# First norm of a conditioned RG-LRU block: scale folded into the input weights, shift into a bias per channel

## The reference

```python
cond = jax.nn.silu(c)
mod = cond @ ada_w[0] + ada_b[0]              # 6 * 1024 columns
sh1, sc1, g1, sh2, sc2, g2 = jnp.split(mod, 6, axis=-1)
hn = rmsnorm(x, norm1_g[0]) * (1.0 + sc1[:, None, :]) + sh1[:, None, :]
# rglru_mixer(hn, ...)
u = h @ w_in
gate_br, x_br = u[..., :LRU_WIDTH], u[..., LRU_WIDTH:]
x_br = causal_dwconv(x_br, conv_w, conv_b)    # 4 taps
# two gates: sigmoid of x_br @ wa, x_br @ wx, block by block of 128 channels
# a = exp(-8 r softplus(-lam)), b = sqrt(1 - a^2) * (i * x_br), hs = scan of a, b over the tokens
y = hs * jax.nn.gelu(gate_br, approximate=True)
```

## Time and profile before

| | us |
|---|---|
| median of three runs | 1261.25 |
| lowest and highest | 1256.77, 1261.7 |
| the profiled execution | 1262.1 |
| its span, first to last instruction | 1260.4 |
| TensorE busy | 1093.1 (87%) |
| VectorE busy | 768.6 (61%) |
| ScalarE busy | 650.0 (52%) |
| GpSimd busy | 611.9 (49%) |

### The profile page before, as it was taken

One profiled execution on the slowest core, in us unless ns is written; L12 is line 12 of the kernel. 1 busy time (PEld: TensorE's weight loads), 2 busy tenths in 40 slices (PEclk: granted clock), 3 DMA queues, 4 the chain that ended last, 5 costly groups with the idle time before them and its releaser, 6 DMA issues. The chain is left out here.

```text
span 1260.4 us, 18928 instructions
## 1 busy us (share of the span) xinstructions
PE 1093.1 (87%) x4857; PEld 850.4 (67%) x4858; DVE 768.6 (61%) x1198; ACT 650.0 (52%) x900; POOL 611.9 (49%) x665
## 2 busy tenths in 40 slices
PE   2797999999999997379999992599799999999991
PEld 2686788888888885368888871476466666766660
DVE  3477866667657664536677778356456655656541
ACT  3988766776677666322222212255556655555541
POOL 0061726637447340022567767146555655666553
PEclk9788999999999999689999995699999999999996
DMA  9550334433343312661445627857687887776751
GB/s 362 194 193 29 107 102 135 154 117 121 118 156 118 117 51 83 220 231 69 152 179 189 234 118 267 271 191 252 222 297 245 288 299 245 261 250 231 246 168 51
DMA packets 130871, 231.00 MB, mean 183 GB/s; under 512 B 24104, under 2 KB 91776, under 8 KB 129296
## 3 DMA queue, kind: packets, MB, share of 16 engines
q1 hardware_dynamic: 88976, 118.15, 28.2%
q0 software_dynamic: 23632, 62.49, 13.5%
q10 hardware_dynamic: 18224, 49.90, 11.6%
HBM read 175.87 MB, written 91.31 MB: 212 GB/s over the span
## 5 line engine op out<-in xcount | busy, mean ns | idle before, releaser
L1687 PE MATMUL po<-w_dn,e_ah 128*128 (+1 forms) x312 | 147.1, 616 | 16.9 <-issue 8.9
L1666 PE MATMUL pl<-w_hi,e_xh 128*128 (+1 forms) x312 | 140.9, 452 | 11.8 <-DVE e_xl L1577 6.3
L1210 PE MATMUL po<-wo_hi,b_yh 128*128 128x512 f32 x256 | 105.0, 410 | 28.0 <-DVE wo_lo L1024 28.0
L1668 PE MATMUL pl<-w_hi,e_xl 128*128 (+1 forms) x312 | 124.7, 400 | 0.0
L1667 PE MATMUL pl<-w_lo,e_xh 128*128 (+1 forms) x312 | 124.0, 397 | 0.0
L558 DVE SCALAR_TENSOR_TENSOR XB<-xu,v_cols,XB 128x512 f32<-128x512 f32 x96 | 90.1, 939 | 43.2 <-ACT XB L336 39.5
L1687 PEld LDWEIGHTS po<-w_dn,e_ah 128*128 128x128 f32 x312 | 57.9, 195 | 80.0 <-issue 80.0
L1377 POOL TENSOR_TENSOR e_ob<-e_obs,e_fg 128x1024 f32<-128x1024 f32 x38 | 91.1, 2397 | 32.2 <-ACT e_obs L1495 32.2
L674 PE MATMUL pg<-hT_hi,wg_hi 128*128 128x512 f32 x256 | 103.1, 403 | 0.0
L1211 PE MATMUL po<-wo_lo,b_yh 128*128 128x512 f32 x256 | 101.6, 397 | 0.0
L1212 PE MATMUL po<-wo_hi,b_yl 128*128 128x512 f32 x256 | 101.6, 397 | 0.0
(11 more groups left out here) (287 smaller groups left out, 2637.4 us busy)
## 6 DMA issues: line engine op xcount, KB each, us to landing
e_xg<-hn_slots ACTq DMA_DIRECT2D x40, 512.0 KB, 5.4
e_xa<-x_slots ACTq DMA_DIRECT2D x38, 512.0 KB, 3.8
stg<-in_ada_w_dram POOLq DMA_DIRECT2D x32, 512.0 KB, 4.2
w_raw<-in_moe_w_down_dram SPq DMA_DIRECT2D x16, 1024.0 KB, 7.3
w_raw<-in_moe_w_gate_dram SPq DMA_DIRECT2D x32, 384.0 KB, 4.3
w_raw<-in_moe_w_up_dram SPq DMA_DIRECT2D x32, 384.0 KB, 5.7
n_ada<-in_ada_w_dram ACTq DMA_DIRECT2D x4, 2048.0 KB, 18.4
hn_slots<-in_x_dram SPq DMA_DIRECT2D x16, 512.0 KB, 5.4
```

The source lines that it names most:

```text
L1210: nc.tensor.matmul(po[u][:, hcols], yh[u][:, tok], wo_hi[:, k, hcols], start=(k == 0), stop=False)
L1666: nc.tensor.matmul(gu[:], xh[:, tok], hi, start=(k == 0), stop=False)
L1668: last = nc.tensor.matmul(gu[:], xl[:, tok], hi, start=False, stop=(k == KD - 1))
L1687: last = nc.tensor.matmul(dst, ah[:, k * P:(k + 1) * P], rows, start=(k == 0), stop=(k == KF - 1))
```

## The change

hn @ W is written as (x * rstd) @ (scale * W) + shift @ W. So the tiles no longer get scale and shift; the input weights of each channel are multiplied by scale, and shift @ W becomes a bias of 128 numbers per channel and branch. In particular:

- zT and finish_group are gone. ScalarE copies the turned bank straight to the high part (high), VectorE subtracts it from the bank for the low part (low). A bank is free for the next turn only when low is done.
- Per channel and branch VectorE makes weights times shift (into a scratch that lies over stg for channel 0 and over GE later), weights times scale in place (scale_weights), and a reduction over k of the first (bias_sums). TensorE sums that over the partitions (bias_column, one product of width one), ScalarE copies it to SBUF. The bias enters in the copy of px to xu and in the gelu.
- convert waits for the scaled weights. The gelus wait until the scratch over GE is free.
- SP loads the condition rows and the first channel's weights first and holds the x tiles back until the third quarter of the table has landed. The small decay constants move ahead of the tiles.
- Tiles 4 to 15 are scaled in place by VectorE (tensor_scalar, 128x1024) and turned by a transpose in place of the product with a diagonal. There are four diagonals in place of two.
- TensorE turns five tiles ahead of the first projection (twelve before), three behind each of the first two, five behind the first g projection. A projection of fresh tokens waits once for its whole group. The first gates wait for all 16 low parts. GpSimd starts its table loads when the g bias sums of channel 0 are done.

```diff
 def turn(it):
     pe.wait_ge(diag_ready, 2 * it + 2)
     if it >= 2:
-        pe.wait_ge(zT_ready, it - 1)
+        pe.wait_ge(lo_ready, it - 1)
...
+                if it < FIRST_SCALED:
+                    last = nc.tensor.matmul(dst, rows, diag[:, it % NDIAG], start=True, stop=True)
+                else:
+                    last = nc.tensor.transpose(dst, rows, cst["ident"][:])
...
             def convert(br, j):
-                act.wait_ge(raw_in[br], 16 * (j + 1))
+
+                act.wait_ge(prepared, 6 * j + (2 if br == "x" else 5))
                 nc.scalar.activation(whi[br][:], raw[br][:], ACT.Copy).then_inc(hi_done[br], 1)
...
+            def low(it):
+                dve.wait_ge(hi_ready, it + 1)
+                toks = slice(it * P, (it + 1) * P)
+                nc.vector.tensor_tensor(hT_lo[:, :, toks], pt[it % 2][:].rearrange("p (k n) -> p k n", k=KD),
+                                        hT_hi[:, :, toks].bitcast(F32), ALU.subtract).then_inc(lo_ready, 1)
...
+                nc.vector.tensor_tensor(shifted[not at_least(j, 1)][:], raw[br][:], by_key(shift), ALU.mult).then_inc(prepared, 1)
+                dve.wait_ge(prepared, i + 1)
+                nc.vector.tensor_tensor(raw[br][:], raw[br][:], by_key(scale), ALU.mult).then_inc(prepared, 1)
...
+                nc.vector.tensor_reduce(part[:], shifted[not at_least(j, 1)][:].rearrange("p k n -> p n k"), AX.X, ALU.add).then_inc(prepared, 1)
...
                     if before:
                         finish(hh)
+                    if h == 0 and not last:
+                        if before:
+                            dve.wait_ge(y_ready, hh)
+                        scale_weights("x", j + 1)
+                        bias_sums("x", j + 1)
                     if h == 1:
                         mod_row(j)
+                        if not last:
+                            dve.wait_ge(y_ready, hh)
+                            scale_weights("g", j + 1)
+                            bias_sums("g", j + 1)
...
                     else:
-                        pe.wait_ge(zT_ready, NT - 1)
+                        pe.wait_ge(lo_ready, NT)
```

More of the change, by code:

```diff
@@ L213, in _ @@
             load_bias(0)
-            for it in range(XR, NT):
+            sp.wait_ge(ada_in[2], 16)
+            for it in range(NT):
                 load_tile(it)
@@ L290, in gates_out @@
+            high(7)
+            squares(8)
+            squares(9)
             def gates_out(c, n, j):
@@ L311, in decay, with gelus @@
                 nc.scalar.activation(M[:], A[:], ACT.Square).then_inc(sq_ready, 1)
-            def gelus(hh, first):
+            def gelus(hh, j, first, later):
+                if later is not None:
+                    act.wait_ge(prepared, later)
                 for n in range(NH):
@@ L510, in _ @@
             nc.vector.tensor_scalar(sp_t[:, 0], lam, -1.0, 0.0, ALU.mult, ALU.max).then_inc(s_b, 1)
+            weigh(4)
             dve.wait_ge(s_b, 9)
@@ L516, in _ @@
             nc.vector.tensor_scalar(gb, gb, 0.5, None, ALU.mult).then_inc(s_b, 1)
+            weigh(5)
+            diagonal(0)
+            diagonal(1)
+            weigh(6)
+            weigh(7)
+            diagonal(2)
+            diagonal(3)
+            low(0)
+            low(1)
+            columns()
+            scale_weights("x", 0)
+            low(2)
+            bias_sums("x", 0)
+            low(3)
+            diagonal(4)
+            low_weights("x", 0)
+            diagonal(5)
+            low(4)
+            diagonal(6)
+            low(5)
+            scale_weights("g", 0)
+            diagonal(7)
+            low(6)
+            bias_sums("g", 0)
+            low_weights("g", 0)
+            low_gates(0)
+            low(7)
+            diagonal(8)
+            diagonal(9)
             def finish(hh):
@@ L583, in body @@
                         scan_input(hh - 1)
+                    if begins and h == 0:
+                        low(8)
+                        low(9)
+                        diagonal(10)
+                        diagonal(11)
                     low_xb(c, 0)
```

253 lines of the change are left out of this document (132 added, 121 removed).

## The result

The changed kernel takes 1279.7 us (median of four runs, 1277.49 to 1284.12), where the kernel before takes 1259.01 beside it: a ratio of 1.0174, with a 95% interval from 1.0125 to 1.0223. The forecast was 1274.5, with a range from 1255 to 1286. The profiled execution of the changed kernel took 1277.49 us, with a span of 1275.5.

The account below looks back on a forecast made before the run. TensorE's row of matmuls was taken to bound the seven-channel stretch. Span 1260.4 + 1.3 (front) + 12 (passages) = 1273.7, with 1.7 around it 1275.4, less 0.85 for the median: 1274.5 us, range 1255 to 1286.

Parts of the forecast that it names:

- the passage: From one channel to the next: late g weight conversion and bias columns cost 1.7 us, seven times, +12 us.
- the 4 to 18: Bounds in us on the +12 us forecast for all seven channel-to-channel passages together.
- T: Start of a channel's fourth gate product on TensorE; for channel 0 forecast at 143.5 us, 142.15 before.
- The front: Channel 0 up to its fourth gate product: first projection 16 us ahead, lead then spent, net +1.3 us (-5 to +4).
- the +1.3: Forecast change in us of channel 0's time to its fourth gate product, range -5 to +4.
- the sum: Front's addition to channel 0's fourth gate product: 110.8 + 8.3 + 24.1 = 143.2 us, taken as 143.5.
- the ring of tiles 11 to 15: Front, behind the g projection: five tiles at about 2.5 us each over TensorE, ScalarE, VectorE; last low part at 110.8.
- VectorE's two jobs per tile: Front: per tile VectorE does scaling, 0.9 us, and low part, 1.15 us; cited against an early start surviving.
- (a): Rival: channel passage hidden, 4 us or less from the passages, time 1262; chance 0.20.
- (b): Rival: front's early start survives, channel 0's fourth gate product at 134.5, -8 us, time 1258 or 1253; chance 0.15.
- (c): Rival: in the passage both products wait out a GpSimd instruction, 2 us more per passage, +14, time 1288; chance 0.12.
- (d): Rival: x tiles end the front's weighings, sums start only at 45, front +6, time 1280; within the forecast's 0.53.

Follow-up runs that it names:

- the run with the old loads: Changed kernel with the loads in the order of the kernel before and no wait for the table's third quarter: 1270.5 us, ratio 1.0104 to the kernel before.
- the run with the three orders: Changed kernel with the order of channel 0's front changed on VectorE, ScalarE and TensorE, same work: 1271.1 us, ratio 1.0088 to the kernel before.
- the run with GpSimd held: Changed kernel with GpSimd's addition held in channels 0 to 6 until VectorE's two g weight products are done: 1290.1 us, ratio 1.0236 to the kernel before.

## Why the prediction was right, and where it was off

**Side and mechanism were right.** The largest term was the passage: the conversion waits for two products, the chain behind it is late, TensorE waits on XBl. Taking the wait away, taking the work away and adding the wait alone to the kernel before each moved the period by 1.6 to 1.9 us, and the same work of the x branch moved it by nothing, as the prediction had it: hidden in VectorE's idle time.

**The size of the passage was off**: 1.7 us were put down for it and 2.26 measured, 15.8 us in all instead of 12, still inside the 4 to 18. Of that, 1.4 were put down for the late gate product, the g bias column included, and it came 2.12 late. The first mis-sized term is the second product: 1.22 to 1.45 us were taken from the earlier trace rows, and it took 2.21, since GpSimd's addition starts beside the first one; the tanh was at T + 4.94 instead of 4.0 to 4.4. The second is what stands between tanh and first tap: 0.35 was put down for the bias column's copy and its wait, and 0.66 came, of which 0.42 is from that copy's start to the next; gelu and copy of px with a bias take the rest. The low part XBl shrank to 0.69 as foreseen. The reduction took 2.05 us instead of 1.22. Its elements lie 128 apart and those of the earlier trace rows side by side, which may be the reason and was not tested; it stands behind the conversion's release and cost nothing. The other part of the passage, 0.3 for the x bias column, is 0.24 (a period of 52.57 against 50.21 is 2.36 in all); the seventh passage, which ends in the last channel, costs 1.8, and so the mean is 2.26.

**The front was right to 0.4 us, in good part by luck.** First projection 55.9 (57 was said), second 75.05 (75.7), first gate product 109.63 (110.8), T 143.87 (143.5). T of channel 0 scatters by 2 us with the same code, and the baseline of 142.15 is one of two that lie 3.65 apart, so a hit to 0.4 us, and the +1.3 beside +1.72, say little. Inside it errors cancelled. The sums started 1.35 us later than said. One term that was put at nothing belongs here: SP's issue of a gate weight block was to hold its queue no longer than the third quarter of the table takes to land, and it held it until 23.21, about 2.5 us behind that quarter's landing (about 20.7), so the tiles were issued only from 24.06. The sums then took 4.98 us and not 6.83, the first gate product came 1.2 us ahead of the sum, and from the first to the second gate product it took 8.52 us instead of the 6.9 in the sum, at a granted clock of 0.80. From there to T the sum has 25.5 and the trace 25.72. What the prediction did not ask is what else the lead could have been: it took the load order as what makes the sums early, and the run with the old loads shows that it delays them. It called the ring of tiles 11 to 15 and VectorE's two jobs per tile the price of the lead; the run with the three orders shows that some 9 us of it were order, not work.

**The rivals.** (a) fell: a wait of 1.25 us is in every rolled channel. (b) fell for this kernel; with the front in order T is 134.42, the -8 of that rival. (c), the port, was named as a rival with 2 us per passage and was half right: one of the two products waits, for 1.0 us. Its condition, that both wait, did not come, since the first product goes ahead and GpSimd waits for it. (d) was true in part: the tiles did hold up the last two weighings, by 7.10 us, but the sums started at 39.55 and not at 45, and the load order behind it is worth 3.4 to 4.7 us of T, less than the 6 it was given.

**The rest.** Behind the channels the profiled execution was 2.4 us shorter, and 5.6 us of the difference of the medians are in none of the profiled terms; the prediction had no term for the experts' scatter, which is larger than its own error of 5.2 us.

## What to carry to other kernels

Before work is put in front of a conversion or a copy, list what is queued behind that instruction on its engine: here two products cost 1.9 us per channel only because a tanh, a decay, two gelus and the taps stood behind the conversion, and half a channel earlier the same product was free. Put work where the trace shows the engine idle, and change the order on all engines of a ring at once: VectorE's alone gained nothing, three engines together some 9 us. And look at what the third engine will run beside after the move: holding GpSimd back by 2.4 us won 1.0 us at the conversion and lost 2.25 us of the period. Last, compare an order of the front over several executions, since a single one scattered by 2 us.

## What the runs showed of the hardware that was not expected

- A product of 128x1024 takes 1.20 us beside GpSimd's addition of 128x512 if it starts first (the addition then takes 2.32 instead of 1.29), and the next one takes 2.21. In two programs the figures agree to 0.01 us.
- Idle times of 1.25 and 1.41 us on TensorE left the granted clock at 1.00. Of five of 2.3 to 2.4 us in the same place, in the run with GpSimd held, four were followed by 4.1 us at a mean of 0.58 or 0.59 and cost 1.6 us more; behind the fifth, of 2.44 us, the clock stayed at 1.00. One of 1.92 us, ahead of the last channel's first gate product, was followed by the same low clock.
- The same code of the front gave 142.56 to 144.62 us for T in five kernels; the column sums alone took between 3.73 and 4.98 us there, and 6.83 at a granted clock of 0.50 in the kernel before.
- A reduction of 128x1024 over elements 128 apart takes 1.90 us alone and 2.03 to 2.05 in the passage, against 0.95 for 768 elements per partition side by side.
- SP's issue of a gate weight block held its queue for 14.95 us here, and one of the g weights for 18.07 with the old loads, while the table was in flight:

```profile
8.26 14.95 SPq L156 DMA_DIRECT2D gate_w<-in_lru_wa_dram  x1
```
